# Chunk 0 of the next block's first panels enters as two parts, and the fourth panel ahead is split in four pieces

## The reference

```
n   = rmsnorm(h, g_in)
out = block(n)                       # FFN: (silu(n @ w_gate) * (n @ w_up)) @ w_down
h   = h + res * rmsnorm(out, g_out)  # res 0.5 for an FFN of the first layers, else 1
```

## Time and profile before

| | |
|---|---|
| runs | 1433.89, 1434.93, 1434.78 us; median 1434.78 |
| profiled execution: span | 1436.0 us; the page has no other time of it |
| TensorE busy | 1419.0 us, 99%, 10988 products |
| VectorE, ScalarE, GpSimd busy | 947.8, 662.0, 45.6 us (66%, 46%, 3%) |
| mean granted clock of TensorE | 0.998 of full speed |
| the chain that ended last | PE 92%, DVE 3%, ACT 2%, DMA 2%, issue 1% |
| DMA | 233.99 MB, 52.4% of 16 engines' time |

### The profile page before, as it was taken

The page is one execution under the profiler, slowest core; times in us unless marked ns, Lnnn a source line. Parts: engine busy times, 40 slices in busy tenths (PEclk is TensorE's granted clock), DMA queues, the critical chain, the costliest instruction groups (busy, mean ns, idle before and its releaser), DMA issues.

```text
span 1436.0 us, 26258 instructions
## 1 busy us (share of the span) xinstructions
PE 1419.0 (99%) x10988; PEld 1361.9 (95%) x10988; DVE 947.8 (66%) x1223; ACT 662.0 (46%) x876; POOL 45.6 (3%) x72
## 2 busy tenths in 40 slices
PE   9999999999999999999999999999999999999998
PEld 9999999978999999999999988999999997999887
DVE  6656568566865555866557677876656975787653
ACT  5444345544544343544435357544444555544432
POOL 0000010010000000000001000000001010000000
PEclk9999999999999999999999999999999999999999
DMA  7586765511455576455454640465656540356552
GB/s 219 177 226 186 206 195 161 176 61 60 147 176 175 173 217 200 147 176 175 145 168 157 205 147 2 146 206 176 191 175 205 172 152 30 119 176 208 187 195 99
DMA packets 238904, 233.99 MB, mean 163 GB/s; under 512 B 29791, under 2 KB 233492, under 8 KB 238816
## 3 DMA queue, kind: packets, MB, share of 16 engines
q1 hardware_dynamic: 238024, 232.33, 52.4%
q10 hardware_dynamic: 792, 0.40, 0.1%
HBM read 231.52 MB, written 1.12 MB: 162 GB/s over the span
## 4 chain that ended last, share of the span: by engine, by line
PE 92%; DVE 3%; ACT 2%; DMA 2%; issue 1%; DVEq 0%; SPq 0%; ACTq 0%
PE acc L646 22%; PE acc L647 22%; PE acc L648 22%; PE acc L709 4%; PE aux L876 2%; PE aux L875 2%; PE aux L874 2%; PE acc L715 2%; PE aux L646 2%; PE aux L647 2%; PE aux L648 2%; PE aux L941 1%; PE acc L1154 1%; ACT w_hi L1400 1%; PE acc L1262 1%
## 5 line engine op out<-in xcount | busy, mean ns | idle before, releaser
L646 PE MATMUL acc<-x_hi,w_hi 128*128 128x272 f32 (+1 forms) x1960 | 559.8, 286 | 1.6 <-DVE z L1999 0.9
L647 PE MATMUL acc<-x_lo,w_hi 128*128 128x272 f32 (+1 forms) x1960 | 559.6, 286 | 0.0
L1856 DVE TENSOR_TENSOR w_lo<-raw,w_hi 128x2048 fp32r<-128x2048 f32 (+1 forms) x229 | 482.0, 2109 | 117.3 <-ACT w_hi L1400 116.6
L648 PE MATMUL acc<-x_hi,w_lo 128*128 128x272 f32 (+1 forms) x1960 | 557.9, 285 | 0.0
L1400 ACT ACTIVATE w_hi<-raw 128x2048 fp32r<-128x2048 f32 (+3 forms) x251 | 407.0, 1627 | 171.1 <-DMA raw<-in_ffn_w_down 52.7
L646 PEld LDWEIGHTS acc<-x_hi,w_hi 128*128 128x128 f32 x1960 | 369.4, 188 | 4.5 <-issue 1.7
L647 PEld LDWEIGHTS acc<-x_lo,w_hi 128*128 128x128 f32 x1960 | 368.2, 188 | 0.3 <-issue 0.2
L648 PEld LDWEIGHTS acc<-x_hi,w_lo 128*128 128x128 f32 x1960 | 368.3, 188 | 0.0
L646 PE MATMUL acc<-hid_hi,w_hi 128*128 128x272 f32 (+1 forms) x704 | 201.9, 287 | 0.0
L647 PE MATMUL acc<-hid_lo,w_hi 128*128 128x272 f32 (+1 forms) x704 | 201.6, 286 | 0.0
L648 PE MATMUL acc<-hid_hi,w_lo 128*128 128x272 f32 (+1 forms) x704 | 200.7, 285 | 0.0
(11 more groups left out here) (340 smaller groups left out, 1610.5 us busy)
## 6 DMA issues: line engine op xcount, KB each, us to landing
raw<-in_ffn_w_gate SPq DMA_DIRECT2D x44, 1024.0 KB, 5.4
raw<-in_ffn_w_up SPq DMA_DIRECT2D x44, 1024.0 KB, 5.4
raw<-in_ffn_w_down SPq DMA_DIRECT2D x32, 768.0 KB, 4.9
raw<-in_ffn_w_down SPq DMA_DIRECT2D x32, 640.0 KB, 4.4
raw<-in_w_up SPq DMA_DIRECT2D x16, 1024.0 KB, 5.4
raw<-in_w_down SPq DMA_DIRECT2D x16, 1024.0 KB, 4.8
raw<-in_na_w_qkv SPq DMA_DIRECT2D x12, 1024.0 KB, 5.2
raw<-in_da_w_qkv SPq DMA_DIRECT2D x12, 1024.0 KB, 5.3
```

The lines of the kernel that those rows point to most:

```text
L646: nc.tensor.matmul(o, wh, xh, start=first, stop=False)
L647: nc.tensor.matmul(o, wh, xl, start=False, stop=False)
L648: return nc.tensor.matmul(o, wl, xh, start=False, stop=last)
L1856: nc.vector.tensor_tensor(w_lo[:, slot, w], raw[:, slot, w], w_hi[:, slot, w].bitcast(F32), ALU.subtract)\
```

## The change

The passage's first chunk is not summed before it is multiplied. gain * (h0 * sd + y0) goes to TensorE as two summands: y0 times the next block's gain (`y_hi`, `y_lo`, made in `y_parts` by VectorE at the down phase's local panel 12, a mixer's panel 1), and h0 * gain * sd (`part_hi`, one VectorE operation once sd is there, and `part_lo`). The products of the former, 12 (`first_y`), stand in `sum_rest` in place of `keep_warm`: two between the sums, ten behind them. The products of the latter are chunk 0's; its high ones come first, its low ones behind chunk 1's high ones. The stream's own chunk 0 is made by GpSimd (`first_residual`, two operations on 128 x 272), and its x_hi and x_lo, which panels from 2 on use, are made last of the eight.

In passages 0, 2, 3 and 5 the second of the panels used together (panel 1) is split in four pieces of 512 columns by `high_piece` and `low_piece`, which stand between the squares of the last halves, behind sd, and in `residual`, instead of whole at local panel 13. The addition of the third last square is one VectorE operation (`post_sum`) in all passages, so that TensorE has two sums and not three in the FFNs' too.

Semaphores count accordingly (h_ready, scaled_ready: seven chunks a passage; SyncE's waits on them likewise, and one on `first_done`). The new tiles lie in the memory of z. Cut to its core, added and removed lines only:

```diff
# TensorE: first_panels, first_y
-    for k in range(DC):
-        shared_chunk(n, SPLIT_IN[k_], tokens, k)
+    pe.wait_ge(part_ready, 2 * k_ - 1)
+    shared_high(n, tokens, 0, part_hi[:, 0:tokens], False)
+    pe.wait_ge(x_hi_ready, SPLIT_IN[k_] + 1)
+    shared_high(n, tokens, 1, x_hi[:, 1, 0:tokens], False)
+    pe.wait_ge(part_ready, 2 * k_)
+    shared_low(n, tokens, 0, part_lo[:, 0:tokens])
+    pe.wait_ge(x_ready, SPLIT_IN[k_] + 1)
+    shared_low(n, tokens, 1, x_lo[:, 1, 0:tokens])
+    for k in range(2, DC):
+        shared_chunk(n, SPLIT_IN[k_] - 1, tokens, k)
+    pe.wait_ge(x_ready, SPLIT_IN[k_] + 8)
+def first_y(k_, tokens, products):
+    n = 2 * k_ + 2
+    ph = PHASES[n]
+    for at in products:
+        j, m, part, ys = ([(j, m, *kind) for j in range(2) for m in range(2)
+                           for kind in ((w_hi, y_hi), (w_lo, y_hi), (w_hi, y_lo))])[at]
+        if at == 0:
+            pe.wait_ge(w_lo_ready, ph.p0 + 1)
+            pe.wait_ge(acc_free, ph.a0 - 1)
+            pe.wait_ge(y_split, 2 * k_ + 2)
+        if at == (3 if k_ == NA else 6):
+            pe.wait_ge(acc_free, ph.a0)
+        if at == 6:
+            if k_ in (NA, DA, MIX):
+                pe.wait_ge(w_lo_ready, ph.p0 + 2)
+            else:
+                pe.wait_ge(lo_piece, pieces_before(k_) + 1)
+        nc.tensor.matmul(banks(n, 0, j)[:, m, 0:tokens], part[:, (ph.p0 + j) % SLOTS, m * P:m * P + P],
+                         ys[:, 0:tokens], start=at % 3 == 0, stop=False)
...
+        pe.wait_ge(x_hi_ready, base + k + 1)
+        shared_high(n, tokens, k, x_hi[:, k, 0:tokens], k == 0)
+        pe.wait_ge(x_ready, base + k + 1)
+        shared_low(n, tokens, k, x_lo[:, k, 0:tokens])
+def shared_high(n, tokens, k, xs, first):
...
-        pe.wait_ge(x_hi_ready, base + k + 1)
...
+            in_pieces = n % 2 == 0 and j == 1 and n // 2 - 1 not in (NA, DA, MIX)
+            if in_pieces and k % 2 == 0:
+                if k < 6:
+                    pe.wait_ge(lo_piece, pieces_before(n // 2 - 1) + k // 2 + 1)
+                else:
+                    pe.wait_ge(w_lo_ready, ph.p0 + 2)
...
-                pe.wait_ge(w_lo_ready, ph.p0 + j + 1)
+                if not in_pieces:
+                    pe.wait_ge(w_lo_ready, ph.p0 + j + 1)
...
# TensorE: sum_rest
-    if k_ in (NA, DA, MIX):
-        pe.wait_ge(post_summed, mixer_count(k_) + 1)
-    pe.wait_ge(sq_added, additions(2 * k_ + 1) + 3)
+    pe.wait_ge(post_summed, k_ + 1)
...
-    if k_ not in (NA, DA, MIX):
-        pe.wait_ge(sq_ready, squares_before(2 * k_ + 1) + 4)
-        nc.tensor.matmul(ps_post[:, 0:tokens], ones[:, :], sq[:, 1, 0, 0:tokens], start=False, stop=False)
+    first_y(k_, tokens, range(2))
...
-    if k_ < MLP:
-        keep_warm(aux[:, 0, :], 8)
+    first_y(k_, tokens, range(2, 12))
...
# ScalarE: high_piece, boundary
+def high_piece(n, piece):
+    ph = PHASES[n]
+    slot = (ph.p0 + 1) % SLOTS
+    size = FULL * CW // 4
+    w = slice(piece * size, piece * size + size)
+    if piece == 0:
+        act.wait_ge(raw_full[slot], ((ph.p0 + 1) // 4 + 1) * 16)
+    nc.scalar.activation(w_hi[:, slot, w], raw[:, slot, w], ACT.Copy)\
+        .then_inc(hi_piece if piece < 3 else w_hi_ready, 1)
...
+    n = 2 * k + 2
+    in_pieces = k not in (NA, DA, MIX)
...
+    if in_pieces:
+        high_piece(n, 0)
+        high_piece(n, 1)
...
+    if in_pieces:
+        high_piece(n, 2)
...
-    n = 2 * k + 2
-    for c in range(DC):
-        high_part(k + 1, c)
-        if c % 2:
-            high(n, 0, 2, c // 2, 4)
-            square(n, c // 2, h[:, c - 1:c + 1, 0:tokens], tokens)
+    if in_pieces:
+        high_piece(n, 3)
+    for pair in range(4):
+        for c in (2 * pair, 2 * pair + 1):
+            if c > 0:
+                high_part(k + 1, c)
+        high(n, 0, 2, pair, 4)
+        if pair == 1:
+            act.wait_ge(first_done, 2 * k + 2)
+            square(n, 0, h[:, 0:2, 0:tokens], tokens)
+        if pair == 3:
+            high_part(k + 1, 0)
+        if pair > 0:
+            square(n, pair, h[:, 2 * pair:2 * pair + 2, 0:tokens], tokens)
...
# ScalarE: output_steps
-            if k not in (NA, DA, MIX):
-                high(n, i, j + 4)
...
# VectorE
-    dve.wait_ge(scaled_ready, DC * k + c1)
+    dve.wait_ge(scaled_ready, (DC - 1) * k + c1 - 1)
...
+def low_piece(n, piece):
+    ph = PHASES[n]
+    slot = (ph.p0 + 1) % SLOTS
+    size = FULL * CW // 4
+    w = slice(piece * size, piece * size + size)
+    if piece < 3:
+        dve.wait_ge(hi_piece, pieces_before(n // 2 - 1) + piece + 1)
+    else:
+        dve.wait_ge(w_hi_ready, ph.p0 + 2)
+    nc.vector.tensor_tensor(w_lo[:, slot, w], raw[:, slot, w], w_hi[:, slot, w].bitcast(F32), ALU.subtract)\
+        .then_inc(lo_piece if piece < 3 else w_lo_ready, 1)
+def post_sum(k):
+    tokens = SUBS[k][4]
+    dve.wait_ge(sq_ready, squares_before(2 * k + 1) + 4)
+    dve.wait_ge(sq_added, additions(2 * k + 1) + 3)
+    nc.vector.tensor_tensor(sq_sum[:, 0, 0:tokens], sq_sum[:, 0, 0:tokens], sq[:, 1, 0, 0:tokens],
+                            ALU.add).then_inc(post_summed, 1)
+def y_parts(k):
+    tokens = SUBS[k][4]
+    gain = gains[:, SUBS[k + 1][0]:SUBS[k + 1][0] + 1]
+    dve.wait_ge(acc_free, PHASES[2 * k + 1].a0 + 1)
+    nc.vector.tensor_scalar(h_gained[:, 0:tokens], h[:, 0, 0:tokens], gain, None, ALU.mult)
+    nc.vector.tensor_scalar(y_hi[:, 0:tokens], y[:, 0, 0:tokens], gain, None, ALU.mult).then_inc(y_split, 1)
+    dve.wait_ge(y_split, 2 * k + 1)
+    nc.vector.scalar_tensor_tensor(out=y_lo[:, 0:tokens], in0=y[:, 0, 0:tokens], scalar=gain,
+                                   in1=y_hi[:, 0:tokens].bitcast(F32), op0=ALU.mult, op1=ALU.subtract)\
+        .then_inc(y_split, 1)
+def part_low(k, tokens):
+    gain = gains[:, SUBS[k + 1][0]:SUBS[k + 1][0] + 1]
+    dve.wait_ge(part_ready, 2 * k + 1)
+    dve.wait_ge(first_done, 2 * k + 1)
+    nc.vector.scalar_tensor_tensor(out=part_lo[:, 0:tokens], in0=h[:, 0, 0:tokens], scalar=gain,
+                                   in1=part_hi[:, 0:tokens].bitcast(F32), op0=ALU.mult, op1=ALU.subtract)\
+        .then_inc(part_ready, 1)
...
+    in_pieces = k not in (NA, DA, MIX)
+    if in_pieces:
+        post_sum(k)
...
+        if in_pieces and m == 0:
+            low_piece(2 * k + 2, 0)
+            low_piece(2 * k + 2, 1)
...
-    scale_h(k, 0, 1)
-    add_y(k, 0, 1)
+    nc.vector.tensor_tensor(part_hi[:, 0:tokens], h_gained[:, 0:tokens], sd[:, 0:tokens], ALU.mult)\
+        .then_inc(part_ready, 1)
...
-    if k < MLP:
-        low_part(k + 1, 0)
...
-        if k < MLP and q > 1:
+        if q > 1:
...
-        if k < MLP:
-            low_part(k + 1, 2 * q - 1)
-    if k == MLP:
-        return
+        if q == 1:
+            part_low(k, tokens)
+        elif in_pieces:
+            low_piece(2 * k + 2, q)
+        low_part(k + 1, 2 * q - 1)
...
+    low_part(k + 1, 0)
...
# VectorE: output_steps
+        if local == (1 if k in (NA, DA, MIX) else 12) and k < MLP:
+            y_parts(k)
...
-            if k not in (NA, DA, MIX):
-                low(n, i, j + 4)
...
-            dve.wait_ge(sq_ready, squares_before(2 * k + 1) + 4)
-            dve.wait_ge(sq_added, additions(2 * k + 1) + 3)
-            nc.vector.tensor_tensor(sq_sum[:, 0, 0:tokens], sq_sum[:, 0, 0:tokens], sq[:, 1, 0, 0:tokens],
-                                    ALU.add).then_inc(post_summed, 1)
+            post_sum(k)
...
# GpSimd
+def first_residual(k, tokens):
+    pool.wait_ge(sd_ready, 2 * k + 2)
+    nc.gpsimd.tensor_tensor(h[:, 0, 0:tokens], h[:, 0, 0:tokens], sd[:, 0:tokens], ALU.mult)\
+        .then_inc(first_done, 1)
+    pool.wait_ge(part_ready, 2 * k + 2)
+    nc.gpsimd.tensor_tensor(h[:, 0, 0:tokens], h[:, 0, 0:tokens], y[:, 0, 0:tokens], ALU.add)\
+        .then_inc(first_done, 1)
...
# GpSimd, once for every k below 7
+        first_residual(k, SUBS[k][4])
```

More of the change, by code:

```diff
@@ L213, in program @@
         gathered = sb("gathered", [P, 2, 2, P], F32, c)
+        c = [z_at]
+        h_gained = sb("h_gained", [P, NT], F32, c)
+        y_hi = sb("y_hi", [P, NT], F32R, c)
+        y_lo = sb("y_lo", [P, NT], F32R, c)
+        part_hi = sb("part_hi", [P, NT], F32R, c)
+        part_lo = sb("part_lo", [P, NT], F32R, c)
+        assert c[0] <= z_at + 8 * NT * 4
         c = [z_at + 2 * NT * 4]
@@ L317, in program @@
         w_lo_ready = sem("w_lo_ready")
+        hi_piece = sem("hi_piece")
+        lo_piece = sem("lo_piece")
         panel_used = sem("panel_used")
@@ L329, in program @@
         sum_ready = sem("sum_ready")
+        y_split = sem("y_split")
+        part_ready = sem("part_ready")
+        first_done = sem("first_done")
         sd_ready = sem("sd_ready")
@@ L500, in squares_before, with h_before, pieces_before @@
             return 9 * (event // 2) + 4 * (event % 2)
-        def mixer_count(k):
-            return (NA, DA, MIX).index(k)
+        def h_before(k):
+            return DC + (DC - 1) * (k - 1)
+        def pieces_before(k):
```

(19 more changed lines are left out.)

## The result

The kernel got slower: 1445.08 us in the median of four executions (1442.49 to 1445.13) against 1434.75 before. The medians lie 10.3 us apart; the ratio on record is 1.0057 (95% interval 1.0042 to 1.0072), which is 8.2 us. A second measurement (after_again) gave 1.0043 (1.0030 to 1.0056), 6.1 us between its medians. The forecast was 1436.7 with a range of 1430.8 to 1440.6. The profiled execution has a span of 1443.2 us, 7.2 more than before.

The account below looks back on a forecast made before the run. TensorE, 99% busy, bounds the kernel, with VectorE's chain level at the fifth panel. Losses 1.15, 1.15, 0.1, 0.1, 1.1 less gains 0.25, 0.7, 0.65 give 1.9 us later: 1436.7 us median, range 1430.8 to 1440.6.

Parts of the forecast that it names:

- T: Start of the first sum on TensorE in a passage between blocks; restart forecast 2.5 us later in all seven.
- chunk 1 stalls: TensorE's wait ahead of chunk 1's products after part_hi: 0.3 us, becoming 0.8 with GpSimd's first operation.
- panel 14: Block 0's panel 14, whose split stands behind y_parts on VectorE without slack: 1.1 us later (bounds 0.9 and 1.4).
- A: Start of VectorE's first whole w_lo split after the stream parts; forecast T + 12.5 (mixers) or T + 13.1.
- A + 17.0: Start of the fifth panel in passage 1, where VectorE's chain and TensorE arrive together; forecast 29.5 us behind T.
- A + 5.1: End of VectorE's add of halves, behind which the third panel's sum holds TensorE in passages 0, 3, 5 and 6.
- GpSimd's turns: GpSimd's two h0 operations inside VectorE's chain, each delaying VectorE's next operation: taken as 0.45 us twice a passage.
- sd: ScalarE's result after the second sum, which starts VectorE's list in each passage; forecast at T + 1.96.
- Passage 6: Last of the seven passages, taken as held by the third panel's sum: 17.05 against 16.95, 0.1 us later.
- The clock: TensorE's clock, said to stay at full speed, so that only gaps and added products count.
- Rival C: VectorE's chain does not hold TensorE, all stalls are its own: 5.5 us faster, 1429.3; chance 0.07.
- B: Rival: GpSimd gets in front of part_hi and each turn costs 0.57: 5 us, 1441.7; chance 0.18.

Follow-up runs that it names:

- after_again: The changed kernel itself, unchanged, measured a second time against the kernel before: ratio 1.0043 (1.0030 to 1.0056).
- gpsimd_one_column: Changed kernel with GpSimd's two operations on h0 cut to one column (leaves work out, to measure only): 1.0003 of the kernel before.
- h0_on_vector: Changed kernel with h0 x sd and h0 + y0 on VectorE instead of GpSimd: 1.0038 of the kernel before.
- y_parts_later: Changed kernel with y_parts behind the w_lo split instead of ahead of it in the FFN output stages: 1.0039 of the kernel before.
- short_lists: Changed kernel, GpSimd's h0 operations and VectorE's last two square adds cut to one column, y_parts later, panel 3's w_hi earlier: 0.9949 of the kernel before.

## Why the prediction was wrong

The picture was right. TensorE runs without a gap from T to the part_hi products and restarts at T + 2.36 to 2.68 (forecast 2.5); chunk 1 stalls 0.65 to 0.70 (0.8); panel 14 costs 1.07 (1.1); A + 17.0 still gives the fifth panel in passage 1 (12.89 + 16.98) and 2, A + 5.1 the sum in 0 and 3. What failed is the price of what was added to VectorE's list, and the slack that was assumed behind it:

- **GpSimd's turns**, "I take 0.45 twice": they cost 0.58 twice (gpsimd_one_column), above the bound of 0.57 (0.54 at 256 columns). That is about 0.26 a passage, 1.8 us in all. VectorE's scale starts at 370.44, 0.08 before part_hi ends, and lasts 1.01. GpSimd's operation lasts 1.03; the 0.6 us of it that lie behind part_hi's end are about the 0.58 that VectorE loses. This is the rule of the Trainium skill (SBUF — State Buffer, "Who interferes with whom") that whoever comes first holds the port pair that VectorE and GpSimd share for the whole instruction, and the other waits. I had set it aside for rows in which part of the operation seemed to overlap; by it the sum would have been some 2.5 us later. The measurement is nearer to the page. The nearest row was no counterexample: GpSimd's operation there was itself shorter, 0.85 us against 0.98 here at the same 256 columns, and VectorE's loss was smaller by as much, 0.41 against 0.54.
- **sd**, "With sd at T + 1.96": by the prediction's own rows VectorE sees it at 367.45 - 365.42 = 2.03, and after the change too (370.08 - 368.05). That is 0.07 a passage, 0.5 us. Together with GpSimd's turns it makes A come 0.3 to 0.4 later than forecast in every passage (13.40, 12.88, 13.39, 13.50, 12.34, 12.97, 12.28), 2.3 to 2.4 us in all.
- **Passage 6**, "k = 6: sum 17.05 against 16.95, 0.1 later": 1.43 later. I gave it the slack of the passages that are held by the sum alone. There the fifth panel waits for its own w_lo:

```profile
1278.82 2.28 DVE L1939 TENSOR_TENSOR w_lo<-raw,w_hi 128x2048 fp32r<-128x2048 f32 x1
```

  It ends 15.6 us behind A (1265.52), and the panel starts 0.14 later, A + 15.7. Before, A + 15.7 was 26.5, just the 26.57 of the earlier trace rows: no slack. The list held this passage as it held 1 and 4.
- **Block 6**: passage 5's gain of 0.17 and 0.56 more is lost at a panel that waits 0.52 for its w_lo. I did not look for the next wait behind the fifth panel.
- **The clock**, "the clock stays at full speed": it does not, the profiled execution of the kernel before has the stretch at 902 to 906 us. I did not price what the longer wait in passage 4 sets off either. The low clock follows it in all four profiles with a wait of 1.85 us or more there (after, after_again, h0_on_vector, y_parts_later) and in none with 1.66 or less; 1.5 us. In the profile the two stretches cancel. In the medians they need not: the four executions of the kernel before took under 1435 us, and in the later sets all five executions of it under 1435 have a mean clock of 0.999 or 1.000. The stretches' 6.2 us and this 1.5 are 7.7 of the ratio's 8.2. That the four had no such stretch is not shown, since their clocks are not on record.

The forecast's terms add up to 2.0 us, not 1.9. The profile has 7.2. Of the 5.2 between them, 3.5 lie between T and the fifth panel (+0.9 forecast, +4.4 measured: 1.8 for GpSimd's turns, 0.5 for sd, 1.1 for the rest of passage 6, 0.1 other), 0.7 in block 6 and 1.0 at the start. Rival C is refuted (gpsimd_one_column, short_lists), and so is B's order: VectorE is first by 0.04 us in all seven passages (370.08 against 370.12 in passage 1). Only B's price was right, and its time of 1441.7 is nearer to the result for another reason.

## What to carry to other kernels

A restart of TensorE that comes 1.1 us earlier is worth something only if the engine that feeds it from there on has slack; here VectorE's list ran level with TensorE, and the change lengthened it. Where an operation is moved to GpSimd beside a VectorE list of operations that read two SBUF tensors, count on VectorE's list the time that GpSimd still needs when VectorE's own operation has ended, and compare that with what VectorE needs for the work (0.58 against 0.36 here). Follow the list past the first wait that you know to the next ones: where TensorE and VectorE come together with no wait shown, there is no slack.
